# Gated-branch decoder step in split fp32 on one core: the low parts of twelve down-projection chunks, from a subtraction on VectorE to a negated copy and an accumulating transfer

## The reference, cut to what matters

```python
hn = rmsnorm(h, norm_ffn)
h = h + (jax.nn.silu(hn @ w_ff_gate) * (hn @ w_ff_up)) @ w_ff_down   # 1024 -> 2816 -> 1024
...
y_prompt = rmsnorm(hp, norm_final)
```

## Time and profile before

| | |
|---|---|
| three runs | 1069.89, 1070.38, 1071.01 us (median 1070.38) |
| profiled execution | 1069.33 us, span 1067.6 us |
| PE | busy 1057.3 us, 99% of the span |
| DVE | 718.2 us, 67% |
| ACT | 479.7 us, 45% |
| POOL | 110.8 us, 10% |
| granted TensorE clock | 0.997 over the span |
| HBM | 122.34 MB read, 7.54 MB written |

### The profile page before, as it was taken

The page is one execution under the profiler, slowest core; times in us unless marked ns, Lnnn a source line. Parts: engine busy times, 40 slices in busy tenths (PEclk is TensorE's granted clock), DMA queues, the critical chain, the costliest instruction groups (busy, mean ns, idle before and its releaser), DMA issues.

```text
span 1067.6 us, 20526 instructions
## 1 busy us (share of the span) xinstructions
PE 1057.3 (99%) x8751; PEld 1051.1 (98%) x8751; DVE 718.2 (67%) x1234; ACT 479.7 (45%) x550; POOL 110.8 (10%) x93
## 2 busy tenths in 40 slices
PE   9999999999999999999999999999999999999997
PEld 9999999999999999999999999999999999999996
DVE  6766677888888654686323755578778457588754
ACT  6744443453335353344345723344456245366431
POOL 3661000002300000000000000000000000000000
PEclk9999999999999999999999999999999999999998
DMA  8967886689796878758876663231578365487512
GB/s 293 289 189 190 222 208 154 195 228 316 215 274 140 208 172 195 177 148 192 207 187 158 160 237 116 81 99 40 152 185 198 114 148 145 119 199 176 169 41 80
DMA packets 151194, 187.25 MB, mean 175 GB/s; under 512 B 4759, under 2 KB 141295, under 8 KB 145591
## 3 DMA queue, kind: packets, MB, share of 16 engines
q1 hardware_dynamic: 117734, 106.64, 31.8%
q0 software_dynamic: 8496, 57.15, 26.7%
q10 hardware_dynamic: 24880, 22.26, 6.9%
HBM read 122.34 MB, written 7.54 MB: 122 GB/s over the span
## 4 chain that ended last, share of the span: by engine, by line
PE 96%; DVE 3%; ACT 0%; issue 0%; POOL 0%; DVEq 0%; POOLq 0%
PE acc L2218 39%; PE acc L2236 20%; PE acc L2592 12%; PE acc L2544 11%; PE acc L2551 6%; PE acc L2329 2%; PE acc L2190 2%; PE acc L2337 1%; PE acc L2433 1%; PE acc L2409 1%; DVE o_acc L1631 0%; DVE ubyb L1462 0%; DVE yA L1693 0%; PE acc L2494 0%; DVE w_l L1337 0%
## 5 line engine op out<-in xcount | busy, mean ns | idle before, releaser
L2218 PE MATMUL acc<-big_h,w_h 128*128 128x260 f32 x1664 | 337.2, 284 | 0.1
L2218 PE MATMUL acc<-big_l,w_h 128*128 128x260 f32 x1664 | 334.4, 282 | 0.0
L2218 PEld LDWEIGHTS acc<-big_h,w_h 128*128 128x128 f32 x1664 | 255.8, 188 | 0.7 <-DVE st L1667 0.3
L2218 PEld LDWEIGHTS acc<-big_l,w_h 128*128 128x128 f32 x1664 | 256.4, 189 | 0.0
L2236 PE MATMUL acc<-big_h,w_l 128*128 128x260 f32 x1664 | 209.0, 283 | 0.0
L2236 PEld LDWEIGHTS acc<-big_h,w_l 128*128 128x128 f32 x1664 | 203.7, 189 | 0.1
L1462 DVE SCALAR_TENSOR_TENSOR ubyb<-ubyb,prm 128x512 f32<-128x512 f32 (+1 forms) x240 | 180.3, 751 | 15.1 <-DVE ubyb L1462 9.4
L749 ACT ACTIVATE w_h<-w_raw 128x1024 fp32r<-128x1024 f32 x120 | 120.2, 1051 | 103.5 <-DMA w_raw<-in_w_out_a_dram 29.7
L2544 PE MATMUL acc<-x_h,ws_h 128*128 128x260 f32 x504 | 126.0, 282 | 0.0
L2544 PE MATMUL acc<-x_l,ws_h 128*128 128x260 f32 x504 | 125.8, 282 | 0.0
L2544 PEld LDWEIGHTS acc<-x_h,ws_h 128*128 128x128 f32 x504 | 94.9, 188 | 0.2
(11 more groups left out here) (278 smaller groups left out, 1327.8 us busy)
## 6 DMA issues: line engine op xcount, KB each, us to landing
w_l<-w_raw POOLq DMA_DIRECT2D x41, 1024.0 KB, 8.1
w_raw<-in_w_in_dram SPq DMA_DIRECT2D x36, 1024.0 KB, 5.3
ws_l<-w_raw POOLq DMA_DIRECT2D x18, 768.0 KB, 7.4
w_raw<-in_w_ff_gate_dram SPq DMA_DIRECT2D x18, 512.0 KB, 5.0
w_raw<-in_w_ff_up_dram SPq DMA_DIRECT2D x18, 512.0 KB, 4.9
k_st<-in_cache_mem_k_dram ACTq DMA_DIRECT2D x8, 1024.0 KB, 8.2
v_st<-in_cache_mem_v_dram ACTq DMA_DIRECT2D x8, 1024.0 KB, 12.6
w_raw<-in_w_v_dram SPq DMA_DIRECT2D x4, 1024.0 KB, 8.0
```

The costliest lines, as they stand in the source:

```text
L2218: last = M.matmul(out[:, b, 0:HALF], w_h[:, slot, k, cols], xs[:, k_at + k, b * HALF:(b + 1) * HALF], start=start and k == 0 and xs is x[0 ...
```

## The change

The low part of s = 15 to 18, 23 to 26 and 34 to 37 is made by a negated copy on ACT (one instruction for the whole chunk, after the two halves of the high part) and an accumulating transfer that POOL issues, of 512, 768 or 1024 KB. VectorE's `down_low` and its four calls go. PE's low products wait for the whole transfer, not for halves. SP reloads a slot of `w_raw` when the transfer has ended, no longer when the subtraction has. `rests` and `los` count anew.

```diff
 def rests(s):
-    return 16 * sum(is_seven(n) for n in range(s % 2, s + 1, 2))
+    return 16 * sum(SEVEN <= n for n in range(s % 2, s + 1, 2))
...
 def los(s):
-    return 2 * (s - SEVEN)
+    return 2 * sevens(s)
...
                 elif s >= SEVEN:
-                    sp.wait_ge(st_lo, los(s) + 2)
+                    sp.wait_ge(st_rest[s % 2], rests(s))
+                    sp.wait_ge(st_hi, his(s) + 2)
...
             for s in range(SEVEN, S_END):
-                if is_seven(s):
-                    pool.wait_ge(st_neg, sevens(s) + 1)
+                pool.wait_ge(st_neg, s - SEVEN + 1)
+                if is_down(s):
+                    kn = PARTS[ORDER[s][1]][1]
+                    pool.dma_start(wd_l[s % 2][:, 0:kn, :].rearrange("p k n -> p (k n)"),
+                                   w_raw[:, s % 2, 0:kn, :].rearrange("p k n -> p (k n)"),
+                                   accum_op=ALU.add).then_inc(st_rest[s % 2], 16)
+                else:
                     pool.dma_start(ws_l[s % 2][:, 0:3, :, :].rearrange("p b r n -> p (b r n)"),
...
                     nc.scalar.activation(wd_h[s % 2][:, ks, :], w_raw[:, s % 2, ks, :], ACT.Copy).then_inc(st_hi, 1)
+                nc.scalar.activation(wd_l[s % 2][:, 0:2 * half, :], w_raw[:, s % 2, 0:2 * half, :], ACT.Copy, scale=-1.0) \
+                    .then_inc(st_neg, 1)
...
-            def down_low(s):
-
-                half = PARTS[ORDER[s][1]][1] // 2
-                for h in range(2):
-                    ks = slice(h * half, (h + 1) * half)
-                    if h == 0:
-                        set_free(s)
-                    dve.wait_ge(st_hi, his(s) + h + 1)
-                    V.tensor_tensor(wd_l[s % 2][:, ks, :], w_raw[:, s % 2, ks, :], f(wd_h[s % 2][:, ks, :]), ALU.subtract) \
-                        .then_inc(st_lo, 1)
...
                 elif n < SEVEN:
                     plain_low(n)
-                else:
-                    down_low(n)
...
             down_add(S_LAST)
-            down_low(S_LAST + 2)
             rows_out(0)
             square_sum(1)
             down_add(S_LAST + 1)
             rows_out(1)
-            down_low(S_LAST + 3)
...
-                                pe.wait_ge(*((w_own, own(C_F + s) - 2 + h) if plain else (st_lo, los(s) + h)))
+                                pe.wait_ge(*((w_own, own(C_F + s) - 2 + h) if plain else (st_rest[slot], rests(s))))
```

## The result

The changed kernel takes 1082.84 us (median of four runs, 1082.39 to 1083.85) against 1070.65: a ratio of 1.0115, 95% interval 1.0101 to 1.0129, so 12.3 us more where 5.2 were forecast, and outside the range. The way was right, the size was not. Its profiled execution took 1083.12 us with a span of 1081.4.

The account below looks back on a forecast made before the run. The prediction took PE, busy for 99% of the span, as the bound. Its terms, 4.2 + 0.5 + 0.5 = +5.2 us, on the median of 1070.38 gave 1075.6 us, range 1071.0 to 1081.5.

Parts of the forecast that it names:

- Nothing but PE sets the time, and taking work from VectorE can give nothing back: Whole kernel before the last product: removing 24 subtractions of VectorE is worth 0, at most 0.5 us.
- More than PE's own wait counts SP's: Slots of w_raw: free only once their transfer lands, so the load of chunk s + 2 starts later, beside another transfer.
- Load of 28 ... 0.5 beyond: Load of s = 28: starts at 934.5, lands 942 to 944.2 where 941.8 is allowed, 0.5 us booked.
- 8 us, 875.5: Load of s = 20: starts at 867.5 beside the transfer of 19, 875.2 allowed; 0.5 us booked, between 0 and 2.0.
- The step before it: Transfer of s = 26: issued at 927.9 beside the load of 27, lands 934.5, PE asks at 934.84; just in time.
- at D chunks of 4 tiles themselves: Sign of a wrong forecast: PE waits at these chunks, so the 512 KB transfer exceeds 6 us and all terms grow.
- Load of 27 ... 1.9 us late: Load of s = 27: issued at 927.1, 7.5 us in flight, lands 934.6 where 932.7 is allowed; 1.9 us late.
- transfer of 27 ... 1.5: Transfer of s = 27: beside the load of 28, lands 943.8 where PE asks at 942.5; 1.5 us booked.
- s = 37: Last 1024 KB transfer, 7.2 us: lands 1042.95, PE asks at 1042.49; 0.5 us booked, between 0.1 and 1.4.
- The clock: Rival: waits of 2 us in a row tip PE's clock, one F chunk at half speed costs 10 us, 1085.6; chance 0.04.
- The loads starve and stay late: Rival: loads beside a transfer take 9.7 us each time at four places, lateness 11.9 us, 1082.3; chance 0.13.
- The spare time holds: Rival: transfers and loads land at undisturbed times, 4.5 and 5.8 us; 0 to 2 us more, about 1071.0; chance 0.19.

Follow-up runs that it names:

- mix: Changed kernel with the new way only for s = 15, 16, 17, 23, 24, 34, 35, 36, subtraction for 18, 25, 26, 37: ratio 0.9999 to the kernel before.
- negonly: Kernel before plus the twelve negated copies on ACT, VectorE's subtractions kept behind them, no new transfer: ratio 1.0007.
- only26: Changed kernel with the new way for s = 26 alone, the eleven other D chunks by subtraction: ratio 1.0055 to the kernel before, +5.9 us.
- lateload: Kernel before with the loads of s = 20 and 28 held until PE ended the first half of chunk 18's and 26's output: ratio 1.0115.
- nocollide: Changed kernel with the transfers of s = 19 and 27 cut to 512 bytes per partition: ratio 1.0057 to the kernel before, +6.1 us.
- p1: Changed kernel with the new way only for s = 15 to 18, subtraction for the other eight: ratio 1.0026 to the kernel before, +2.8 us.
- lateslack: Kernel before with the loads of s = 20 and 28 held only until PE ended chunk 17 and 25: ratio 1.0029, +3.1 us.
- sub18_26: Changed kernel with s = 18 and 26 by subtraction again: ratio 1.0044 to the kernel before, +4.7 us.
- p2: Changed kernel with the new way only for s = 23 to 26, subtraction for the other eight: ratio 1.0093 to the kernel before, +10.0 us.
- traffic: Kernel before plus eight more accumulating transfers into SBUF nobody reads then, with no PE or SP wait on them: ratio 1.0014, +1.5 us.
- copyfirst: Changed kernel with ACT's copy and VectorE's first sums of s = 19 and 27 ahead of the next chunk's negation and sums: ratio 1.0072, +7.7 us.

## Why the prediction was wrong

- *"Nothing but PE sets the time, and taking work from VectorE can give nothing back"*: right; mix and negonly show it from both sides.
- *"More than PE's own wait counts SP's"*: right. The mechanism is the one named: the load of 27 went out when it was said to (927.1; it was 930.2 with PE 3.2 us later), and only26, lateload and nocollide show the late load as the cause.
- *"Load of 28 ... 0.5 beyond"* is the step that failed, and *"8 us, 875.5"* for the load of 20 with it. I took about 8 us for each in flight. They took 9.5 and 11.1 (867.12 to 878.2), because each was issued within 1.1 us of a transfer, the case of the earlier trace rows, which I had put at the far end of the range. The waits were 5.5 and 2.0 where I had 0.5 and 0.5. The step before it fed this: I let the transfer of 26 take 6.6 us, it took 8.4; PE waited 1.3 for it, and the load of 28 started 1.8 us later than I had it (939.5 less PE's shift of 3.2, against 934.5). So the load of 28 was 5.8 us beyond its limit and not 0.5: 1.8 of the difference come from the transfer of 26, 1.7 from the load's own flight (9.5 for 7.8), and 1.8 because I had moved the limit by 3.4 us for waits of PE ahead of the copy, of which 1.6 had come.
- The sign for this stood in the prediction: PE waiting *"at D chunks of 4 tiles themselves"*, the 512 KB transfer *"dearer than 6 us"*. It came at s = 26 (1.3 us, a transfer of 8.4). The other sign, a load of 27 over 6.5 us in flight, did not.
- *"Load of 27 ... 1.9 us late"* and *"transfer of 27 ... 1.5"* did not come: the load of 27 took 5.8 us, its undisturbed time, since it was issued 0.85 us ahead of its rival, and PE had the transfer of 27 when it asked. I spread one middle price over all collisions. In this trace the one issued first by 0.85 us or more kept its time and the second paid: 5.8 and 8.4; 7.0 and 9.5. With the load first by 0.3 us both paid, 11.1 and 10.7, and so it was in p1 (0.4 apart, 10.8 and 10.1) and only26 (0.5 apart, 9.9 and 9.2). It is no firm rule: in lateslack the load of 28 was 1.8 us ahead and took 7.4.
- *s = 37*: 0.5 forecast, 1.4 waited. No other DMA moved in those 8.4 us, so the 7.2 I took was too low a price for 1024 KB alone, although s = 34, also alone, took 7.0.
- *The clock* was a rival with 10 us and a chance of 0.04. It fell behind waits of 1.8 us (sub18_26) to 6.1 (p2) in the profiled executions of five of the kernels here, and in those of traffic and mix behind waits of 1.5 and 1.4 us near the start, where nothing is changed. It did not fall behind the 2.0 us in the changed kernel's s = 19, in only26 or in nocollide. It cost 1.8 us, not 10; what the stages of p1, p2, sub18_26 and lateload lost beyond their waits is 1.6 to 2.9 us at each fall. It belonged in the sum of any case with a wait of a few microseconds.
- *"The loads starve and stay late"* (11.9 us, 0.13) comes near the 12.3 in number, and in part by luck. It had all four places late, 2.0 in s = 19, 8.5 in s = 27 and 28 spread over three loads and a transfer, and 1.4 at the end, with the clock at full. Measured were 2.0, 1.3 and 5.5, 1.4, and 1.8 of slow matmuls; the loads of 27 and 29 cost PE nothing.
- *"The spare time holds"* fell with the rest.

Set against the runs, the rule that a load for chunk s + 1 may land 1.65 us after chunk s begins held: 949.0 against 943.2 is 5.8 late for a wait of 5.5, 942.63 against 940.45 in nocollide 2.2 for 2.0. The error was in the flight times, with the waits that follow from them, and in the clock.

What stays open: s = 26 alone cost 5.9 us by the ratio, but the waits of its profiled execution, the shortest of its runs, add up to 3.6. The other runs hint at the rest: two took 1074.1 and 1074.4 us with a mean granted clock of 0.998, two 1077.1 and 1077.2 with 0.995 and 0.994. So the clock probably fell in two of the four and cost them 2.9 us; where it fell is not on record, and one run of copyfirst has 0.994 without being longer. It was not found why the clock fell behind some waits of 2 us and not behind others.

## What to carry to other kernels

When an operation is moved from an engine to a transfer, ask what the transfer reads: that buffer is held until it lands, and the next load into it starts later, beside the next transfer. Price two transfers that are issued within a microsecond of each other at what such a pair took in the trace, not at a middle value; the later one pays, and half a microsecond apart both may. Then ask what small instruction stands behind the late one in its engine's stream, and put the low clock beside any wait of TensorE as long as those here, 1.4 us and more, as a cost that may or may not come.

## What was not expected of the hardware

- An accumulating transfer of 512 KB took 4.5 us when alone, 8.4 beside two loads of 512 KB issued just ahead; one of 1024 KB, alone, took 7.0 us (s = 34) and 8.4 (s = 37). The Trainium skill ("DMA: Bandwidth & Descriptors", Anatomy of one DMA) prices 1024 KB at 4.4 us by its formula; the runs disagree for this kind.
- The granted clock fell to 0.50 after waits of PE of 1.4 (mix), 1.5 (traffic), 1.8 (sub18_26) and 2.0 us (p1), in each 0.8 to 1.2 us after PE was back at work, and stayed full after 2.0 in three other kernels and 2.2 in copyfirst; in the feed-forward stage it came back some 3 to 6 us after PE was at work again.
